# Column sums of the later modulation chunks: TensorE transposes replaced by VectorE block transposes and one product

## What is computed

```python
c_act = jax.nn.silu(c)
for l in range(DEPTH):
    mod = c_act @ w_mod[l] + b_mod[l]
    shift, scale, gate = jnp.split(mod, 3, axis=-1)
    h = rmsnorm(x, norm_gain[l]) * (1.0 + scale[:, None, :]) + shift[:, None, :]
    proj = h @ w_in[l]
...
    x = x + gate[:, None, :] * y
```

## Time and profile before

| what | value |
| --- | --- |
| median of 3 runs | 1844.23 us (1844.16 to 1845.7) |
| profiled execution: first to last instruction (span) | 1842.2 us |
| what lies around the span, taken as the median less the span | 2.0 us |
| PE busy | 1815.0 us, 99% of the span |
| PEld busy | 1480.5 us, 80% |
| DVE busy | 1278.1 us, 69% |
| ACT busy | 963.8 us, 52% |
| mean TensorE clock granted | 0.999 |
| chain that ended last | PE 91%, DVE 4%, DMA 2%, ACT 1%, issue 1% |

### The profile page before, as it was taken

One profiled execution on the slowest core, in us unless ns is written; L12 is line 12 of the kernel. 1 busy time (PEld: TensorE's weight loads), 2 busy tenths in 40 slices (PEclk: granted clock), 3 DMA queues, 4 the chain that ended last, 5 costly groups with the idle time before them and its releaser, 6 DMA issues.

```text
span 1842.2 us, 25457 instructions
## 1 busy us (share of the span) xinstructions
PE 1815.0 (99%) x9817; PEld 1480.5 (80%) x9817; DVE 1278.1 (69%) x1784; ACT 963.8 (52%) x1373; POOL 204.4 (11%) x261
## 2 busy tenths in 40 slices
PE   6999999999999999999999999999999999999998
PEld 3568788888888878888988888888888888888887
DVE  6349989998987778658756544488885466665555
ACT  5345565456365446545644644577764445443464
POOL 1000021001000001100000000045440020021001
PEclk9999999999999999999999999999999999999999
DMA  9999879967976976654465565655555555557552
GB/s 358 389 368 352 304 253 340 318 221 234 343 281 230 382 245 223 214 161 152 148 217 184 184 200 187 197 177 168 167 166 197 185 185 180 189 177 258 179 197 97
DMA packets 194196, 424.11 MB, mean 230 GB/s; under 512 B 7456, under 2 KB 12460, under 8 KB 192940
## 3 DMA queue, kind: packets, MB, share of 16 engines
q1 hardware_dynamic: 192124, 414.15, 66.0%
q10 hardware_dynamic: 1968, 8.54, 1.1%
HBM read 418.45 MB, written 4.21 MB: 229 GB/s over the span
## 4 chain that ended last, share of the span: by engine, by line
PE 91%; DVE 4%; DMA 2%; ACT 1%; issue 1%; SPq 0%; POOLq 0%; ACTq 0%; POOL 0%; DVEq 0%
PE acc L807 27%; PE acc L809 26%; PE acc L808 26%; DVE w_lo L2061 1%; PE tps L850 1%; PE tps L932 1%; DMA raw<-in_w_in 1%; DMA raw<-in_w_mod 1%; DMA proj<-in_w_mod 1%; PE acc L971 0%; PE acc L972 0%; PE acc L973 0%; PE sps L971 0%; PE sps L1070 0%; DVE proj L2196 0%
## 5 line engine op out<-in xcount | busy, mean ns | idle before, releaser
L2061 DVE TENSOR_TENSOR w_lo<-raw,w_hi 128x1024 fp32r<-128x1024 f32 (+1 forms) x572 | 711.3, 1248 | 449.9 <-ACT w_hi L1423 447.3
L1423 ACT ACTIVATE w_hi<-raw 128x1024 fp32r<-128x1024 f32 (+1 forms) x572 | 599.0, 1051 | 749.9 <-PE acc L809 676.3
L807 PE MATMUL acc<-w_hi,ht_hi 128*128 128x512 f32 (+1 forms) x2256 | 890.7, 395 | 0.8 <-issue 0.8
L809 PE MATMUL acc<-w_hi,ht_lo 128*128 128x512 f32 (+1 forms) x2256 | 875.3, 388 | 0.0
L808 PE MATMUL acc<-w_lo,ht_hi 128*128 128x512 f32 (+1 forms) x2256 | 873.4, 387 | 0.0
L809 PEld LDWEIGHTS acc<-w_hi,ht_lo 128*128 128x128 f32 x2256 | 423.4, 188 | 88.1
L807 PEld LDWEIGHTS acc<-w_hi,ht_hi 128*128 128x128 f32 x2256 | 423.7, 188 | 85.3 <-issue 4.3
L808 PEld LDWEIGHTS acc<-w_lo,ht_hi 128*128 128x128 f32 x2256 | 424.2, 188 | 81.8
L2196 DVE SCALAR_TENSOR_TENSOR proj<-raw,vcol,proj 128x1024 f32<-128x1024 f32 x60 | 80.2, 1337 | 3.8
L2196 DVE SCALAR_TENSOR_TENSOR scr<-raw,vcol,scr 128x1024 f32<-128x1024 f32 x60 | 78.9, 1316 | 4.0
L2911 POOL TENSOR_TENSOR scr<-scr 128x128 f32<-128x128 f32 x56 | 31.1, 586 | 156.8 <-DVE scr L2633 156.8
(11 more groups left out here) (353 smaller groups left out, 1529.9 us busy)
## 6 DMA issues: line engine op xcount, KB each, us to landing
raw<-in_w_in SPq DMA_DIRECT2D x203, 1024.0 KB, 5.1
raw<-in_w_mod SPq DMA_DIRECT2D x64, 1024.0 KB, 5.8
raw<-in_w_out SPq DMA_DIRECT2D x32, 1024.0 KB, 5.2
raw<-in_w_mod SPq DMA_DIRECT2D x44, 512.0 KB, 11.5
raw<-in_w_o SPq DMA_DIRECT2D x16, 1024.0 KB, 5.1
raw<-in_w_ple_gate SPq DMA_DIRECT2D x16, 1024.0 KB, 5.1
raw<-in_w_b_out SPq DMA_DIRECT2D x8, 1024.0 KB, 5.1
raw<-in_w_a_out SPq DMA_DIRECT2D x8, 1024.0 KB, 5.0
```

The costliest lines, as they stand in the source:

```text
L807: pe.matmul(o, hi_m, w_hi[:, slot, u, 0:width], start=start, stop=False)
L809: mm = pe.matmul(o, lo_m, w_hi[:, slot, u, 0:width], start=False, stop=stop)
L1423: act.activation(w_hi[:, x % SPL, :, 0:width], raw[:, j, 2 * (x % halves):2 * (x % halves) + 2, 0:width], ACT.Copy).then_inc(hi_ready, 1)
L2061: dve.tensor_tensor(w_lo[:, x % SPL, :, 0:width], raw[:, j, 2 * (x % halves):2 * (x % halves) + 2, 0:width], w_hi[:, x % SPL, :, 0:width]. ...
```

## The change

For chunks 4 to 11 the eight transposes of TensorE go. After piece 7 VectorE does, for each half e of the home (128 x 512), a transpose of all 32 x 32 blocks in place and one sum over the 32 elements within each block, into a small tile `sums` (`mod_fold`, placed by the new table `FOLDS`, sixteen places). TensorE then does one product of 32 columns with a constant matrix `fold`, which adds the four groups of 32 partitions; its result is 128 x 32 in `tps`, each group of partitions holding all columns. VectorE takes the right 32 x 8 of each group with four additions of `b_mod` (`mod_take`). The wait for `raw_read` at the end of piece 7 goes, and a fold has one in its place. `fold` is formed once on VectorE near the start of the program. Sums and takes are in one go for every chunk, and stand at new places.

```diff
@@ -205,6 +205,8 @@
         ktile = proj[:, 0, N_IN:N_IN + S]
         mb = proj[:, 1, N_IN:N_IN + 384]
         st = sb("st", [P, 64])
+        fold = sb("fold", [P, P])
+        sums = sb("sums", [P, 2, 4, 8])
         tmp8 = proj[:, 0, N_IN + 256:N_IN + 272].rearrange("p (m k) -> p m k", m=M)
         bns = proj[:, 0, N_IN + 272:N_IN + 296].rearrange("p (n k) -> p n k", n=4)
         mv = proj[:, 0, N_IN + 296:N_IN + 304].rearrange("p (n k) -> p n k", n=4)
@@ -358,6 +360,7 @@
         pool_passed = sem("pool_passed")
         mod_summed = sem("mod_summed")
         mod_ready = sem("mod_ready")
+        mod_folded = sem("mod_folded")
         mod_taken = sem("mod_taken")
         scale_ready = sem("scale_ready")
         gate_turned = sem("gate_turned")
@@ -564,21 +567,11 @@
             return plan
 
         PLAN = slots_of_chunks()
-        SUMS, TAKES = {}, {}
-        for l in range(DEPTH):
-            for k in range(0 if l else FRONT, NCH + 5):
-                for x, (n, q, slot) in PLAN[l][k][1].items():
-                    if q == 7:
-                        if 8 <= k < 11:
-                            at = k if x == 1 else k + 1
-                            SUMS[l, at, 1], TAKES[l, at, 5] = (n, (0, 1)), (n, (0, 1))
-                        elif k == 11 or k == 12:
-                            SUMS[l, 12, 2], TAKES[l, 12, 6] = (n, (0, 1)), (n, (0, 1))
-                        elif k == 18:
-                            SUMS[l, k, 6] = n, (0, 1)
-                        else:
-                            SUMS[l, k, 7], TAKES[l, k + 1, 3] = (n, (0,)), (n, (0,))
-                            SUMS[l, k + 1, 2], TAKES[l, k + 1, 6] = (n, (1,)), (n, (1,))
+        FOLDS = {(0, 5, 0): (4, 0), (0, 5, 2): (4, 1), (0, 8, 2): (5, 0), (0, 8, 4): (5, 1), (0, 10, 2): (6, 0), (0, 10, 4): (6, 1),
+                 (0, 12, 2): (7, 0), (0, 12, 4): (7, 1), (0, 16, 4): (8, 0), (0, 16, 6): (8, 1), (0, 18, 4): (9, 0),
+                 (0, 18, 5): (9, 1), (1, 4, 0): (10, 0), (1, 4, 2): (10, 1), (1, 8, 4): (11, 0), (1, 8, 6): (11, 1)}
+        SUMS = {(0, 5, 4): 4, (0, 9, 1): 5, (0, 11, 1): 6, (0, 12, 6): 7, (0, 17, 0): 8, (0, 18, 7): 9, (1, 4, 4): 10, (1, 9, 1): 11}
+        TAKES = {(0, 6, 0): 4, (0, 9, 5): 5, (0, 11, 5): 6, (0, 13, 2): 7, (0, 17, 4): 8, (1, 5, 0): 10, (1, 9, 5): 11}
 
         def home(n):
 
@@ -813,14 +806,11 @@
                             if x % 8 in PLAN[l][k][1]:
                                 lo.skip(2)
                             if (l, k, x % 8) in SUMS:
-                                n, parts = SUMS[l, k, x % 8]
                                 if 8 <= k < 12:
                                     pe.wait_ge(qt_ready, qtr.ahead(2))
                                 if k == 12:
                                     pe.wait_ge(rqt_ready, rq.ahead(2))
-                                if k == 18:
-                                    pe.wait_ge(p_lo, 1)
-                                mod_columns(home(n), parts)
+                                mod_columns(SUMS[l, k, x % 8])
                         if side:
                             side(t, x, first)
                 per = {taken: len(halves) // group, lo: len(halves)}
@@ -881,17 +871,15 @@
 
             m_ready = Seen(pe, mod_ready)
 
-            def mod_columns(src, parts):
+            m_folded = Seen(pe, mod_folded)
+
+            def mod_columns(n):
 
                 pe.wait_ge(mod_taken, m_taken.next())
-                m_taken.skip(len(parts) - 1)
-                if 0 in parts:
-                    pe.wait_ge(mod_ready, m_ready.next())
-                for e in parts:
-                    b = e if len(parts) == 2 else 1
-                    for j in range(4):
-                        tr = pe.transpose(tps[:, b, j * P:(j + 1) * P], src[:, e, j * P:(j + 1) * P], ident)
-                tr.then_inc(mod_summed, len(parts))
+                m_taken.skip(1)
+                pe.wait_ge(mod_folded, m_folded.next())
+                pe.matmul(tps[:, 1, 0:32], fold[:, :], sums[:, n % 2, :, :].rearrange("p j t -> p (j t)"), start=True,
+                          stop=True).then_inc(mod_summed, 2)
 
             def spread_keys(n):
 
@@ -2069,8 +2057,10 @@
                             layer_low(pair)
                         if x % halves == 0:
                             m_land[j].skip(16)
+                        if at and here in FOLDS:
+                            mod_fold(*FOLDS[here])
                         if at and here in TAKES:
-                            mod_take(*TAKES[here])
+                            mod_take(TAKES[here])
                         if at and x % 8 in mods:
                             n, q, slot = mods[x % 8]
                             mod_piece(n, q, slot)
@@ -2196,18 +2186,23 @@
                         r = dve.scalar_tensor_tensor(to, src, c_col, to, ALU.mult, ALU.add)
                     r.then_inc(raw_read, 1)
                     own.skip(1)
-                if q == 7:
-                    dve.wait_ge(raw_read, own.ahead(0))
-                    dve.sem_inc(mod_ready, 1)
-
-            def mod_take(n, parts):
-
-                dve.wait_ge(mod_summed, m_sum.next(len(parts)))
-                at = slice(8 * n + 4 * parts[0], 8 * n + 4 * (parts[-1] + 1))
-                src = tps[:, :, :] if len(parts) == 2 else tps[:, 1:2, :]
-                link(dve.tensor_reduce(modc[:, at], src.rearrange("p b (j q) -> p (b j) q", q=P), AX, ALU.add))
-                dve.tensor_tensor(modc[:, at], modc[:, at], v1("b_mod", at.start, at.stop - at.start), ALU.add)\
-                   .then_inc(mod_taken, len(parts))
+            def mod_fold(n, e):
+
+                dve.wait_ge(raw_read, own.ahead(0))
+                squares = home(n)[:, e, :].rearrange("p (t j a) -> p t j a", j=4, a=32)
+                link(dve.transpose(squares, squares))
+                r = dve.tensor_reduce(sums[:, n % 2, :, 4 * e:4 * e + 4].rearrange("p j t -> p t j"), squares, AX, ALU.add)
+                if e:
+                    r.then_inc(mod_folded, 1)
+
+            def mod_take(n):
+
+                dve.wait_ge(mod_summed, m_sum.next(2))
+                for j in range(4):
+                    q = slice(32 * j, 32 * j + 32)
+                    r = dve.tensor_tensor(modc[q, 8 * n:8 * n + 8], tps[q, 1, 8 * j:8 * j + 8], v1("b_mod", 8 * n, 8)[q, :],
+                                          ALU.add)
+                r.then_inc(mod_taken, 2)
 
             root, accs = Seen(dve, root_ready), Seen(dve, acc_taken, 2)
             sqr = Seen(dve, squares_ready)
@@ -2289,6 +2284,8 @@
                                   ht_hi[:, k:k + 2, :].bitcast(F32), ALU.subtract).then_inc(turn_lo, 2)
 
             buckets()
+            link(dve.tensor_reduce(fold[:, 0:32], ident.rearrange("p (i a) -> p a i", a=32), AX, ALU.add))
+            dve.tensor_copy(fold[:, 32:P].rearrange("p (j a) -> p j a", a=32), fold[:, 0:32].unsqueeze(1).broadcast_to([P, 3, 32]))
             for j in range(24):
                 dve.wait_ge(keys_spread, j + 1)
                 if j >= 4:
@@ -2350,7 +2347,7 @@
 
             def gains_of_second(t, x, first):
                 if x == 1:
-                    mod_take(9, (0, 1))
+                    mod_take(9)
                     gains_of_layer(1)
 
             def rows_by_scale(c):
```

## The result

The changed kernel takes 1848.62 us (median of 10 runs) against 1844.2: it is slower by 4.4 us, and the forecast was 1848.5. The ratio is 1.0022, with an interval from 1.0012 to 1.0031; it leaves out one slow run of the kernel before, at 2019.48 us. The profiled execution has a span of 1847.0 us, 4.8 above that of before.

What follows compares the result with a forecast made beforehand. VectorE was taken to bound 65 us of layer 0 (352.88 to 418.39), its added fold work counting beyond idle time: -0.1 + 4.1 + 1.6 - 1.3 = +4.3 us, 1848.5 us against 1844.2; range 1839.0 to 1854.0.

Steps and rivals of the forecast that it cites:

- What TensorE saves: Eight transposes (0.88) replaced by one product of 32 columns (0.23): 0.65 us saved a chunk, 5.2 for eight chunks.
- What VectorE pays: Transpose and sum 0.68 each, a fold 1.56 extra, a take 0.7; about 2.25 us a chunk, some 18 in all.
- Chunk 4: At k = 5 VectorE is 2.9 late, TensorE's index products wait; of 0.65 saved, 0.1 is left.
- Chunks 5 to 7: k = 8 to 13: VectorE gets 6.8 us more, swallows 2.6 idle and 0.1 smaller; costs 4.1.
- Chunks 8 and 9: k = 16 to 18, end of layer 0: VectorE late at the last products of `w_out`, passed to layer 1; costs 1.6.
- Chunks 10 and 11: Layer 1: VectorE has 15 of 68 us idle, so 2 x 0.65 is gained, 1.3.
- The saving comes through: Rival, everywhere: a fold of 0.9 rather than 1.56 fits VectorE's idle time; 1839.0 us, chance 0.15.
- rival 2: Same mechanism at low prices, 1.36 a fold and 0.35 a take: +0.7, 1844.9 us, chance 0.25.
- rival 3: Block transpose slow on VectorE, 1.37, so a fold costs 2.25: +10.7, 1854.9 us, chance 0.15.
- Rival 4: TensorE waits for a sum because the folds come late; given nothing of its own.

Runs made afterwards that it cites:

- the sixteen additions: Changed kernel with each of a take's four 32 x 8 additions cut into four of 32 x 2; timed in one execution only, 1852.21 us.
- the filled wait: Changed kernel with twelve unread products of 512 columns put ahead of TensorE's wait for layer 0's first retention product; median 1847.68 us, span 1846.8.

## Why the prediction was right, point by point

The mechanism came as forecast: VectorE's folds exceed its idle time up to the retention products, TensorE waits there, and it gains where VectorE is idle. That the total fits to 0.1 us is in part luck. By the places in the profiled executions chunk 4 gave 0.35 more than forecast, chunks 5 to 7 cost 1.1 more (5.2 for 4.1), chunks 8 and 9 cost 0.1 less, and chunks 10 and 11 gave 0.15 more.

**What TensorE saves: right.** Chunk 11 moves TensorE by 0.64 (from 5.47 to 4.83 behind before), forecast 0.65.

**What VectorE pays: right within a tenth.** Transpose 0.71 and sum 0.69 for 0.68 each; the fold 1.47 for 1.56, since in place of the waits of 0.10 there are 0.03 and 0.04; the take 0.69 for 0.7. The rule of the Trainium skill on outputs that begin in another group of 32 partitions (VectorE: DVE Perf Modes, Two Vector instructions with no wait between them) agrees with the sixteen additions, 0.07 to 0.09 apart within a group and 0.15 to 0.16 at a change; the inputs change group together with the outputs there, so the run does not tell which of the two does it. The estimate from its section on the three transpose paths, 1.24 us from 311 ns for a square in 16 bits, does not agree: 0.71 was measured.

**Chunk 4: the wait right, its size wrong.** The step took the index products at 198.60 to wait for the index sum that ended at 195.68, and left 0.1 of the saving of 0.65. Now:

```profile
196.82 1.58 DVE L2378 SCALAR_TENSOR_TENSOR proj<-sps,proj 128x128 f32<-128x128 f32 x4
```

```profile
198.15 0.68 PE L1057 MATMUL sps<-scr 64*128 64x128 f32 x3
198.46 0.37 PE L1057 MATMUL sps<-scr 64*128 64x128 f32 x1
```

The second of these lines is the last of the three products in the first, seen by itself. The sum and the products go by two banks (`dots_used` in `index_dots`). The products of the first bank start at 198.15, in front of the sum's end at 198.40; those of the second start at 198.46, 0.06 behind it. Before, both banks' products started together at 198.60, and the next half came 0.86 later (199.46); now it comes 1.16 later (199.31). So 0.30 is lost at this wait, not 0.55, and TensorE keeps 0.45 (0.43 to 0.50 from k = 4 to k = 8 in every profiled execution but the one with the longer takes).

**Chunks 5 to 7: the mechanism right, the sum made of other terms.** They cost 5.2 in the profiled execution and 4.9 by the medians, for 4.1. The step said: 6.8 us more work, 2.6 swallowed, hence the product at 418.43 is 4.1 late. Up to the first retention product, which leaves out chunk 7's take, it had 6.1 of work. From the first `w_lo` of k = 8 to the first masked scores VectorE takes, its idle pieces over 0.2 taken out, 123.4 us before and 128.3 to 128.6 in five executions with all folds: 5.1. The idle 2.6 is swallowed in full where the stall in k = 9 is short, and then the first retention product is 2.0 to 2.2 later than before (390.95 to 391.19 against 388.99), not 4.1: chunk 7's take (0.7) comes only later, the work is 1.0 less, and VectorE shares the lead of 0.5 that chunk 4 gives. What fills the gap is a term that the sum did not have: after a wait of 3.3 to 4.0 us products run at the lower clock. It is 1.6 us in the profiled execution, as the filled wait shows, and 0.9 to 2.1 in the others up to the next half. A second one is the stall in k = 9, which leaves VectorE 1.53 idle in the profiled execution. The product that the step named, that of the third pair of heads in k = 13, starts at 423.33, 4.90 behind 418.43, but TensorE no longer waits there: VectorE's scores for it begin 4.21 later (421.85 against 417.64), and TensorE is later still. The wait of 0.24 that stood there is gone, which with the pipelining gives 0.5 back. So two misses, one term too large and one left out, met near the forecast: that part is luck. That chunks 5, 6 and 7 do not share it evenly (0 with one of them folded, 0.95 more with two, 3.95 more with all three, by subtraction) bears out the step's idea that only what exceeds the idle time counts.

The Trainium skill (TensorE: Matmul & The Clock Gate, HAM oscillation — how this bites in real kernels) tells of waits between groups of products after which the next group starts at half the clock. The runs agree in part: the clock is 0.50 to 0.60 behind 3.34 and 4.00 of idle time, and 1.00 behind 1.64; but in the second execution of the changed kernel, behind 4.01, the first products still ran at 1.00.

**Chunks 8 and 9: right, +1.5 for +1.6.** VectorE reaches the last products of `w_out` at 546.61, 4.77 taken off 541.84, for 541.9. The order is the step's too: TensorE is 5.53 behind before at half 4 of k = 18 (533.00 against 527.47), back at 4.76 behind the layer's last half (544.16 against 539.40), and 6.30 behind at layer 1's first product (558.91 against 552.61). But it meets the late update at 547.89, where it waits 0.73; the gap ahead of layer 1, forecast at 2.5, is 0.88. By the medians chunks 8 and 9 cost about the same.

**Chunks 10 and 11: right**, -1.45 for -1.3; tripled transposes cost nothing there.

**The rivals.** The saving comes through only where VectorE is idle (4, 10, 11: 1842.57), far from everywhere. The low prices of rival 2 did not come, and the transpose is not the slow one of rival 3. Rival 4, a sum that TensorE waits for, got nothing: such a wait did come, in k = 9, yet not for a fold's result but for a copy on ScalarE behind a late load; taking it out does not change the median.

## What to carry to other kernels

Work moved to a helper engine was free here as far as it fitted into that engine's idle time up to the next place where its result is waited for. What went beyond it made the helper late microsecond for microsecond, so pieces of equal size did not share the price evenly. So move such work piece by piece, and put first what lies where the helper idles. A wait of TensorE that grew had two prices here: its length and, at 3.3 to 4.0 us, the slower products behind it.

## What the hardware showed unexpectedly

Idle for 3.34 us at the first retention product, TensorE took 3.82 us from there to the next half, which takes 2.24 otherwise. Idle for 4.00, it took 4.29 (391.09 to 395.38), and the next half still ran slow; idle for 4.01 in the second execution of the changed kernel, it took 3.10. Products whose result nobody reads, put into the wait, held the clock at 1.00 and saved 1.6 us at that place. Whether the stall in k = 9 lowers the clock differed between executions of one kernel (0.56 behind 1.77 of idle time, no slow products behind 1.01), and behind 1.70 at chunk 6's product in the kernel with sixteen additions the clock stayed 1.00. What sets this was not tried.
